# Scan preparation and chunked scan joined into one block, with one depthwise tile moved from VectorE to GpSimd in the projections

## What is computed

```python
pl = hl @ w_in                                   # also for the 256 context tokens
xbc = silu(dwconv(p_state[..., :SSD_CONV_DIM], conv_w, conv_b))    # 5 taps, 2048 channels
xs, bm, cm = split(xbc)                          # 16 heads x 64, 4 groups x 128, twice
dt = softplus(dt_raw + dt_bias)
# for each of two directions, in chunks of 128 tokens (4 chunks: 2 of context, 2 of x):
acum = cumsum(dt * a_neg)
y  = einsum(cb, exp(where(causal, seg, -inf)), xs * dt) + einsum(cc, s_in, exp(acum))
s  = chunk_decay * s + einsum(bm, to_end, xs * dt)
y  = y + d_skip * xs
o_ssd = rmsnorm(y * silu(z))
# beside it, on the other columns of the projection:
u = v * sigmoid(gate)                            # 1024 channels
o_cf = silu(layernorm(dwconv(u, cf_w, cf_b)))    # 31 taps, in rows of 64 for x, in one row of 256 for the context
y = concat(o_ssd, o_cf) @ w_out
```

## Time and profile before

| what | value |
|---|---|
| median of 3 runs | 2579.03 us (2575.17 to 2593.57) |
| the profiled execution: its own time / its span | 2578.96 us / 2577.1 us |
| PE, PEld, DVE, ACT, POOL busy, share of the span | 86%, 70%, 65%, 51%, 11% |
| projections, preparation, scan (us of the span) | to 1117, 1117 to 1163, 1163 to 1270 |
| mean granted TensorE clock of the span | 0.915 of full |

### The profile page before, as it was taken

The page is one execution under the profiler, slowest core; times in us unless marked ns, Lnnn a source line. Parts: engine busy times, 40 slices in busy tenths (PEclk is TensorE's granted clock), DMA queues, the critical chain, the costliest instruction groups (busy, mean ns, idle before and its releaser), DMA issues. The chain is left out here.

```text
span 2577.1 us, 35878 instructions
## 1 busy us (share of the span) xinstructions
PE 2206.6 (86%) x12176; PEld 1808.2 (70%) x12176; DVE 1672.0 (65%) x2793; ACT 1324.9 (51%) x2076; POOL 281.6 (11%) x355
## 2 busy tenths in 40 slices
PE   3999789979987999948887699995889985699993
PEld 3999666679975666646666687784678874577773
DVE  4784235358634379986663499995567754599993
ACT  2563204346423255665543378883476541488882
POOL 0000000000000056556100001101000000011100
PEclk7999899989998999969999699997898888699996
DMA  5454331344432666600011499996221112499991
GB/s 187 165 182 177 98 122 55 127 178 180 171 119 74 247 235 236 230 25 1 17 66 57 155 356 388 390 394 241 82 75 57 58 58 65 163 392 391 395 386 66
DMA packets 127252, 454.94 MB, mean 177 GB/s; under 512 B 13824, under 2 KB 17792, under 8 KB 126976
## 3 DMA queue, kind: packets, MB, share of 16 engines
q1 hardware_dynamic: 116160, 413.14, 43.8%
q0 software_dynamic: 10944, 39.85, 4.1%
HBM read 431.97 MB, written 20.97 MB: 176 GB/s over the span
## 5 line engine op out<-in xcount | busy, mean ns | idle before, releaser
L2464 DVE TENSOR_TENSOR moe_w_lo<-ring,moe_w_hi 128x1024 fp32r<-128x1024 f32 x384 | 463.0, 1222 | 62.2 <-ACT moe_w_hi L2402 57.2
L2402 ACT CAST moe_w_hi<-ring 128x1024 fp32r<-128x1024 f32 x384 | 399.5, 1050 | 147.3 <-PE ps L236 119.8
L234 PE MATMUL ps<-moe_w_hi,moe_own 128*128 128x512 f32 x512 | 214.2, 418 | 12.1 <-DVE moe_own L2471 11.2
L234 PE MATMUL ps<-ffn_h_hi,ffn_w_hi 128*128 128x256 f32 x704 | 203.6, 289 | 16.9 <-DVE ffn_h_lo L353 16.7
L236 PE MATMUL ps<-moe_w_hi,moe_own 128*128 128x512 f32 x512 | 205.0, 400 | 0.0
L235 PE MATMUL ps<-moe_w_lo,moe_own 128*128 128x512 f32 x512 | 205.0, 400 | 0.0
L235 PE MATMUL ps<-ffn_h_lo,ffn_w_hi 128*128 128x256 f32 x704 | 200.8, 285 | 0.0
L236 PE MATMUL ps<-ffn_h_hi,ffn_w_lo 128*128 128x256 f32 x704 | 200.6, 285 | 0.0
L343 DVE TENSOR_TENSOR ffn_w_lo<-ring,ffn_w_hi 128x1024 fp32r<-128x1024 f32 x132 | 155.4, 1219 | 68.7 <-ACT ffn_w_hi L310 68.7
L310 ACT CAST ffn_w_hi<-ring 128x1024 fp32r<-128x1024 f32 x132 | 131.7, 1049 | 93.3 <-PE ps L236 69.2
L234 PEld LDWEIGHTS ps<-ffn_h_hi,ffn_w_hi 128*128 128x128 f32 x704 | 136.4, 194 | 18.4 <-DVE ffn_h_lo L353 17.5
(11 more groups left out here) (477 smaller groups left out, 5472.2 us busy)
## 6 DMA issues: line engine op xcount, KB each, us to landing
ring<-in_weights SPq DMA_DIRECT2D x766, 512.0 KB, 5.4
expert_rows<-moe_y POOLq DMA_DIRECT2D x32, 512.0 KB, 7.0
token_rows<-moe_token_rows SPq DMA_DIRECT2D x6, 512.0 KB, 3.9
sq<-in_cmp_w SPq DMA_DIRECT2D x1, 2048.0 KB
both<-in_x SPq DMA_DIRECT2D x1, 1024.0 KB, 6.0
both<-in_context SPq DMA_DIRECT2D x1, 1024.0 KB, 8.3
out<-both SPq DMA_DIRECT2D x1, 1024.0 KB, 4.8
cols<-in_cols SPq DMA_DIRECT2D x1, 720.5 KB, 9.1
```

Source lines behind the costliest of these rows:

```text
L234: pe.matmul(out, w_hi, x_hi, start=start, stop=False)
L2402: act.copy(w_hi[:, j % WB].rearrange("p h f -> p (h f)"), k.slot(act, first + GU + j, e).rearrange("p a f -> p (a f)")).then_inc(w_rounded, 1)
L2464: dve.tensor_tensor(w_lo[:, j % WB].rearrange("p h f -> p (h f)"), k.ring[:, (first + GU + j) % RING].rearrange("p a f -> p (a f)"), w_hi[ ...
```

## The change

Five things change, all in `even_in` and `ssd`:

1. POOLED becomes (2, 4, 5, 6). Tile 6 has its 31 taps in the projections, by ACT and POOL, so 124 taps are spread over the steps 6 to 39 where there were 93; u of tile 6 lies in `sq` with the others. Tile 7 (now LATE) is the only one done later.
2. `ssd_prep` and `ssd_scan` become one block. What the end of the first block ordered is now ordered by semaphores: cleared, rows_made, kept, ended, decayed.
3. PE turns only the tokens of the chunks 0 and 1 ahead of the units (groups 0 to 5, `FIRST = 6`), and one group of the chunks 2 and 3 behind front(u + 2) of each of the units 0 to 5. ACT keeps that group behind the exponentials of unit u, before the tap. The sums across come before the sums down.
4. EARLY is 6 where it was 16: six taps of tile 7 ahead of the units, the other 25 behind the units 0 to 24.
5. The multiplication by the skip weights (L1706) is gone. When a chunk is first added to (s = 0 and s = 2, 16 units), DVE does two fused multiply-adds of 128x128 out of PSUM instead of one 128x256 addition.

The masks that tile 6's place took are loaded with the first constants.

```diff
-POOLED, PAIRED, ALONE, LATE_ALONE, LATE_POOLED = (2, 4, 5), (0, 1), (3,), 6, 7
+POOLED, PAIRED, ALONE, LATE = (2, 4, 5, 6), (0, 1), (3,), 7
...
-    EARLY = 16
+    EARLY = 6
...
+        GROUPS, FIRST = TT * 3, TT // 2 * 3
+        def group_bank(n):
+            return n % 5 if n < FIRST else 2 + n % 2
...
                 def turn_tokens(n):
                     tt, b = divmod(n, 3)
-                    if n >= 5:
+                    if n >= FIRST:
+                        pe.wait_ge(kept, max(n - 1, 5))
+                    elif n >= 5:
                         pe.wait_ge(kept, n - 4)
...
+                for n in range(4):
+                    turn_tokens(n)
+                pe.wait_ge(la_ready, 1)
...
+                for n in range(4, FIRST):
+                    turn_tokens(n)
+                pe.wait_ge(cleared, 1)
+                pe.wait_ge(rows_made, 1)
+                pe.wait_ge(kept, FIRST)
                 front(0)
                 front(1)
+                pe.wait_ge(ended, 1)
                 for u in range(NU):
                     back(u)
                     if u + 2 < NU:
                         front(u + 2)
+                    if FIRST + u < GROUPS:
+                        turn_tokens(FIRST + u)
...
             @block.scalar
             def _(act):
+                def keep_tokens(n):
+                    act.wait_ge(turned, n + 1)
...
                     ex.then_inc(expd, 1)
-                    if EARLY + u < CFK:
-                        scale_tap(act, EARLY + u, late_added, u).then_inc(late_scaled, 1)
+                    if FIRST + u < GROUPS:
+                        keep_tokens(FIRST + u)
+                    late_tap(EARLY + u)
...
-                late_taps(len(alone))
...
-                for m in range(XS_TILES):
-                    act.mul(y[:, m, :], y[:, m, :], col("ssd_d")[:, m:m + 1])
...
-                    ad = dve.tensor_tensor(yy, yy, k.ps[:, 6 + u % 2, 0:GW].rearrange("p (a l) -> p a l", a=2), ALU.add)
+                    if s % 2 == 0:
+                        for i in range(2):
+                            m = 2 * g + i
+                            ad = dve.scalar_tensor_tensor(y[:, m, tok], y[:, m, tok], skip[:, m:m + 1],
+                                                          k.ps[:, 6 + u % 2, i * P:(i + 1) * P], ALU.mult, ALU.add)
```

More of the change, by code:

```diff
@@ L1314, in gated_input @@
             def gated_input(m):
[L1315 removed]
+                return late_u if m == LATE else u[:, m, :]
             FROM = 6
@@ L1852, in _, with late_tap @@
                         weigh(u // SG + 1)
-                    if EARLY + u < CFK:
-                        pool.wait_ge(late_scaled, u + 1)
-                        add_tap(pool, EARLY + u)
-                        pool.sem_inc(late_added, 1)
+                    take_tap(EARLY + u)
                     if 2 * SG <= u < NU - 2 * SG:
                         fade(u)
+            @block.scalar
+            def _(act):
+                def keep_tokens(n):
+                    act.wait_ge(turned, n + 1)
+                    tt, b = divmod(n, 3)
+                    to = xs_tok[:, tt, b * 512:(b + 1) * 512] if b < 2 else b_tok[:, tt, :]
+                    act.activation(to, k.ps[:, group_bank(n), :], ACT.Copy).then_inc(kept, 1)
+                def late_tap(i):
+                    if i < CFK:
+                        scale_tap(act, i, late_added, i).then_inc(late_scaled, 1)
+                act.activation(aneg[:, :], col("a_log"), ACT.Exp).then_inc(a_ready, 1)
+                act.wait_ge(dt_abs, 1)
+                act.activation(la_flat, la_flat, ACT.Exp, scale=-1.0)
+                act.drain()
+                act.activation(la_flat, la_flat, ACT.Ln, bias=k.ones[:, 0:1]).then_inc(dt_log, 1)
+                for n in range(4):
+                    keep_tokens(n)
+                    late_tap(n)
+                act.wait_ge(across, 1)
+                act.wait_ge(cleared, 1)
+                for d in range(2):
+                    own = slice(d * ROWS_D, d * ROWS_D + SH)
+                    act.copy(ac_t[own, :, :].rearrange("p c l -> p (c l)"), k.ps[own, 5, :]).then_inc(rounded, 1)
+                for n in range(4, FIRST):
+                    keep_tokens(n)
+                act.wait_ge(ended, 1)
+                act.activation(to_end[:, :, :, :], to_end[:, :, :, :], ACT.Exp)
+                act.activation(cdec[:, :, :, :], cdec[:, :, :, :], ACT.Exp).then_inc(decayed, 1)
+                for i in range(4, EARLY):
+                    late_tap(i)
+                for u, (s, d, c, g) in enumerate(units):
+                    act.wait_ge(rows, u + 1)
+                    if u >= 2:
+                        act.wait_ge(summed, u - 1)
+                    for h in range(SREP):
+                        ex = act.activation(seg[:, u % 2, h, :], k.ps[:, u % 2, h * P:(h + 1) * P], ACT.Exp,
+                                            bias=nacum[:, c, d, g * SREP + h:g * SREP + h + 1])
+                    if s:
+                        ex = act.activation(ce[:, u % 2].rearrange("p h l -> p (h l)"), k.ps[:, 2 + u % 2, :], ACT.Exp)
+                    ex.then_inc(expd, 1)
+                    if FIRST + u < GROUPS:
+                        keep_tokens(FIRST + u)
+                    late_tap(EARLY + u)
```

207 lines of the change are left out of this document (76 added, 131 removed).

## The result

The changed kernel takes 2614.54 us in the median (2613.08 to 2621.21, 4 runs), the kernel before on the same chip 2577.10 (2574.75 to 2593.57, 4 runs). The ratio is 1.0134, with a 95% interval of 1.0108 to 1.0160: slower, and outside the range of the forecast. The profiled execution took 2615.89 us, its span is 2614.1 us and its mean granted clock 0.909, where before had 2577.1 and 0.915.

The account below looks back on a forecast made before the run. PE was taken to bound the projections, DVE to have the last word in the preparation; in the scan ACT never waits for turns. -29.7 + 26.2 + 0.7 + 6 = +3.2 on 2578.96 gave 2582.2 us, range 2567 to 2603.

Parts of the forecast that it names:

- The start of the units: Preparation: without DVE's taps the chain is PE, then ACT, so unit 0 starts 29.7 us earlier.
- The first six units: Scan start: ACT waits each unit for PE's turn, a full round; the first eight units lose 26.2 us, bounds 19.6 to 31.
- I take 6.8: First units of the scan: us per round, chosen between 7.8 at PE's lower clock and 5.8 at its upper.
- today's 2.6 each: Scan: the last two of the first eight units were to keep 2.6 us each, together 5.1.
- The projections: Projections: POOL's added taps lengthen DVE's instructions, less slack; loss 6 us with one last tap, bounds 1.3 to 24.
- The 0.44: Projections, steps 16 to 23: share of POOL's remaining time that its added third of taps was said to fill.
- Less the slack: Projections: DVE's idle 0.45 and 0.49 us a step taken off its growth, leaving 2.0 and 1.2 us of loss.
- rival B: Projections: POOL becomes the bound, ACT and weight split wait, PE idles over 20 us; 34 us lost, 2610; chance 0.13.
- The rest of the scan: Later units: taps cost nothing, two fused additions instead of one cost 0.7 us, bounds 0 and 1.5.
- a tap costs nothing there: Scan: PE's work equal in stretches with and without taps, as POOL adds them between DVE's products.
- A: First units: the round trip costs little, units stay at about 3.5 us; 2562.7 us; chance 0.10.
- C: First units loop at the upper clock, losing 20.7 us, projections only the last tap; 2572; chance 0.2 within the main case.

Follow-up runs that it names:

- e1: Changed kernel with all 12 token groups turned and kept ahead of the units, as before the change: 2584.14 us, ratio 1.0022 to the kernel before.
- e2: Changed kernel with ACT keeping each group turned beside the units one unit later, PE's turns unmoved: 2585.39 us, ratio 1.0028 to the kernel before.
- e3: Changed kernel with the 31 taps of tile 6 left out: 2592.97 us.
- e4: Kernel before with only tile 6's taps moved to ACT and POOL in the projections, its two blocks and scan kept: 2594.44 us.
- e6: Changed kernel with 16 of the 31 taps of tile 6 left out: 2607.29 us.
- e9: Changed kernel with POOL's additions left out for every fourth of the projections' 124 taps, ACT still scaling all: 2599.17 us.
- e11: Changed kernel with five unread matmuls on PE before its wait for DVE, once in four units from unit 8 on: 2604.16 us.

## Why the prediction was wrong, point by point

**The start of the units** was right. I had -29.7 us. From the end of the projections unit 0 came 31.3 us earlier. The chain by PE and ACT without DVE's taps is the one that the trace shows. The size fits in part by luck. The last tap's 1.3 us, which I had counted with the projections, lie in this stretch, so by this division I had -28.4. The difference is the sums, which took 1.0 and 5.0 us and not 1.9 and 6.9, as the clock was at its upper level when they began (1.00 from 1144.2 to 1147.2).

**The first six units** had the right mechanism: starts 7.3 to 9.4 us apart, ACT waiting for L1661 behind every unit's exponentials, and the tap and the next unit queued behind it; e1 and e2 show it. The size was off: 26.2 predicted, 34.4 measured. The step that failed is "I take 6.8", the middle between the clocks. The working had 7.8 for the lower one, and it measured 7.3 to 8.0 at a mean clock of 0.59. I had written beside it that PE would be busy less than half the time and that the lower clock was granted where PE did little; the number should have followed that sentence. (PE was busy for 28.5 of the 48 us, 59%, and my own terms for it, 4.7 of 7.8 us, had said so; the clock was the lower one all the same.) Five rounds at 7.75 instead of 6.8 are 4.7 us, the first round (9.4 for 7.7) another 1.7, and the last two units 1.8, as they took 6.9 us and not "today's 2.6 each". Together 8.2, the difference.

**The projections** cost 22.4 us where I said 6 (with 1.3 of the 6 behind the last step), within the bounds of 1.3 to 24 and near their end. The mechanism of the first half was right, and nearly the size. I had DVE's instructions get longer by 0.7 and 0.6 us a step in the steps 16 to 35, 12.8 us; they got longer by 11.3. (The 0.44 is a slip: POOL's added third, 12.4 us, is 0.73 of the 16.98 that POOL has left in the earlier trace rows, not 0.44. With it the sum would have been some 3 us higher.) Three steps failed:

- "Less the slack": I took 0.45 and 0.49 us of every step off. The 20 steps cost 11.1 us, as much as DVE's instructions grew, and DVE's idle time stayed what it was. Forecast 3.2.
- The steps 6 to 15 are not in the sum at all, though 10 of the 34 steps that get taps are there. They cost 6.4 us, with DVE only 0.9 us busier: ACT's scalings wait for POOL, and the weight casts wait behind them. I had this chain in rival B and gave it nothing in my own case.
- The last four steps cost 4.9 where I put 1.2; DVE's work grew by 4.5 there.

e3 and e4 show that the taps of tile 6 cause all of it, e6 that the first taps cost nearly as much as the last, e9 that without POOL's part DVE's busy time doesn't rise. How the loss divides between DVE's longer instructions and ACT's late casts is read from PE's waits; no run separates the two.

**The rest of the scan** cost 15.9 us where I had 0.7, with bounds of 0 and 1.5. The step that failed is that I compared stretches at a clock of 1.00 and took that clock as given, "a tap costs nothing there". The terms I priced were about right (e11 leaves 1.8). What is missing is a term for the clock: some 14 us at the lower level. From the earlier trace rows I could have seen that the clock was 0.50 ahead of the scan and 1.00 in it, with the engine idle for 1.8 us in every group, and put a bound of one dip a group, some 3.2 us each, on it.

**The rivals.** A fell: starts are 7.8 us apart, not 3.5. B had the right sign and nearly the right sum (2610), but with 34 us in the projections and my own 26.2 in the first units; the PE idle time in the projections was 15.8 us, under its mark of 20, and half of the total loss came from the scan. Its mechanism, ACT behind POOL with the weight split behind ACT, is there in part (6.7 us of PE's waits). C fell, as the loop ran at the lower clock. All three losses were put too low, by 8.2, 16.4 and 15.2 us, and nothing but the 1.6 us at the start spoke for the other side; so the range of 2567 to 2603 didn't hold 2614.5.

The sum of the terms as measured is -31.3 + 34.4 + 15.9 + 22.4 = 41.4 us, less 4.5 for the stretches before and behind them (-0.7 and -3.8), which is 36.9.

## What to carry to other kernels

A copy-out put behind an in-order engine's work on unit u, and waiting for something that needs unit u to be finished elsewhere, costs the whole depth of the pipeline, not the copy: place it one unit later (34 us went to 6 by one condition). Where the bounding engine takes a product of a second engine in every step, don't count that one's last few per cent of idle time as room: here work that made DVE's instructions longer was paid in full. Sum over all steps that get the new work, and look at what stands behind it in the program of the engine that waits for it, here the weight casts behind ACT's scalings. When a change lets PE run dry in a place, price the stage at the lower clock, and add what the stages behind it cost if the clock doesn't stay up.

## What the runs showed of the hardware that I had not expected

The dips can fall in step with the loop. With 1.7 to 1.8 us of idle time in every group of four units, the same instructions run in 13.9 us a group at a clock of 1.00 (before) or in 17.1 us with 7 us at 0.53 (e4, with the scan of before). In the changed kernel four dips came in four groups, up to the end of the scan; in e2 and e9 they ended earlier. Each long dip in the later units of these runs began within 2 us behind an idle piece of at least 1.7 us, but not every such piece had one. Five useless matmuls in the idle piece went with a clock of 0.99, and a loop with more work was 14 us faster (one run). What sets off the first dip stays open: e1 has none before 1230, the kernel before has none in the scan of its profile, and no run here varies the history alone.

The cost of POOL's company: a DVE tap of 128x250 f32 with two inputs in SBUF has a mean of 626 ns with 93 taps on POOL and 681 with 124. The durations at either end are the same (415 and about 1010), so it is the share of taps that meet POOL that grew. The median hides this at first and then overdoes it: 476 ns with 93 taps, 492 with 108 (e6), 770 with 124.
